# Heads and chunks of a hybrid decoder layer reordered, with one addition chain and one small inverse on GpSimd

## The chip, the cores and the metric

The kernel runs on one core of a Trainium2 chip. The metric is the device time of one launch in microseconds. The kernel before took 1549.87 us, the median of three runs (1549.57 to 1550.96).

## The reference

One decoder layer for a prompt of 16 learned tokens and 512 others, and for eight sampled sequences with a paged cache of 16 pages each. The layer has a gated delta rule branch and a stick-breaking attention branch, then a merge and an FFN. The change touches the two prompt branches alone.

```python
def sb_weights(z, valid):                       # attention, per head
    log_stay = jnp.where(valid, jax.nn.log_sigmoid(-z), 0.0)
    log_after = lax.cumsum(log_stay, axis=z.ndim - 1, reverse=True) - log_stay
    return jnp.where(valid, jnp.exp(jax.nn.log_sigmoid(z) + log_after), 0.0)

def gdn_chunk(S, xs):                           # delta rule, per chunk
    ...
    sol = lax.linalg.triangular_solve(lmat, rhs, left_side=True, lower=True, unit_diagonal=True)
    u, w = sol[..., :DV_A], sol[..., DV_A:]
    v_new = u - jnp.einsum('bhck,bhkv->bhcv', w, S)
    qk = jnp.einsum('bhid,bhjd->bhij', q, k) * decay
    o = jnp.einsum('bhck,bhkv->bhcv', q * jnp.exp(G)[..., None], S) + jnp.einsum('bhij,bhjv->bhiv', qk, v_new)
    S_new = jnp.exp(g_last)[..., None, None] * S + jnp.einsum(
        'bhck,bhcv->bhkv', k * jnp.exp(g_last[..., None] - G)[..., None], v_new)

def gdn_finish(o, z, norm_w):
    o = o * lax.rsqrt(jnp.mean(o * o, axis=-1, keepdims=True) + EPS) * norm_w.astype(F32)
```

## The kernel before

Everything is written by hand: each engine has its own instruction list, and the lists are tied together by waits on semaphores. The order of the work is the order of each list. Most of the span is weights: tiles of 128 output features run on TensorE as three products of split operands (L1044). Between tiles of the input projection stand two stages that are chains.

**Heads** (`attend`, once for each of TensorE, ScalarE, VectorE and GpSimd). Eight heads of the prompt's attention. Keys are cut into five tiles of 128, and each tile's queries are the later ones only, so a head is five pieces (`SB_PIECES`), 1344 columns in three PSUM banks. Per head: TensorE makes the scores (L1126); ScalarE scales them into `zs` (L1668, three buffers) and takes abs, exp and ln of softplus in `es` (one buffer, L1676 to L1680); VectorE finishes softplus into `sps` (L2151, two buffers); GpSimd masks it (`causal`, L2648, five selects); TensorE sums it over later keys (`later_sums`, L1141: a triangular product within a key tile and, for every later key tile, a product with ones); VectorE subtracts the sums from the scores (L2161); GpSimd masks the result (again L2648); ScalarE exponentiates (L1690); TensorE multiplies with the values (`values`, L1152); ScalarE copies out (L1695). TensorE's list is sums(h), scores(h+2), values(h). VectorE's is subtraction(h), some pages, softplus(h+2).

**Pages.** A page is 128 rows of a sampled sequence's key cache, fetched by SyncE. VectorE multiplies it with the query and reduces it in eight instructions, one for each head (`k_page`, L2096). Pages are handed out to fill VectorE's idle time: about 3.75 for each head of the attention, and 16 of the seventh sequence in the chunks, by `CHUNK_PAGES`. In the chunks they use a ring of three buffers, so page p is fetched after page p-3 was used, in SyncE's list, which also holds `get_inverse(c)` (eight loads of 32x32 blocks into the two buffers that GpSimd zeroed for chunk c), `late_page` (a page of the eighth sequence, after a chunk's query products) and `last_inverse`.

**Chunks** (`chunks`, again once per engine). The 528 prompt tokens are four chunks of 128 and one of 16, eight heads each, in groups g of four heads. The 32x32 inverses of the diagonal blocks are made ahead; for each chunk two levels (s = 32, 64) join them into one inverse U (`levels`): product q1 on TensorE (L1315), copy by ScalarE (L1810), product up (L1325, L1329), subtraction on VectorE (L2329, L2330 for 32; L2335 for 64). GpSimd makes the masked inputs (L2768). The 16x16 inverse of the last chunk is made in chunk 1 by VectorE's `invert_last`: 30 dependent instructions on 8 partitions and a copy (L2216, L2219, L2237), and goes through DRAM by `last_inverse`.

For chunk c (d = c + 1) TensorE's list is: state products "ks" with the keys, transposed keys "tk" of d, state products "qs" with the queries, transposed values "tv" of d, new values "vn" (L1359), decay columns "dc" of d, state update "kv", output part "o2", key-query products "kq" of d, the levels of d, transposes of the normalised output "ot" (L1383), read by ScalarE (L1839). "ot" and "qs" use the same PSUM banks. VectorE's list: R (L2358, subtracts "ks"), "kr" and "bv" of d, pages, S, o, the products "qk" of d, then the norm: sum of GpSimd's squares "ss" (L2388), "ms", and, after ScalarE's logarithm and exponential "rl" and "rt" (L1832, L1834), "rq" and "on" (L2395); then the levels of d with their pages. GpSimd's list: level inputs and masks of d, decay rows of c + 2, the squares "sq" of c (L2802), zeroing for c + 2 (L2723, L2724).

## Time and profile before

| | us |
|---|---|
| median of three runs | 1549.87 |
| profiled execution | 1550.86 |
| its span | 1548.9 |
| TensorE busy | 1413.1 (91%) |
| VectorE busy | 787.1 (51%) |
| ScalarE busy | 509.5 (33%) |
| GpSimd busy | 147.0 (9%) |
| heads, first sums to last values | 218.3 to 333.4 |
| chunks, loop | 549.7 to 679.5 |

The profiled execution took 1550.86 us, of which the span from the first to the last instruction is 1548.9. Busy times are of one engine over the whole span and overlap. In the rows PE is TensorE, DVE VectorE, ACT ScalarE, POOL GpSimd, and SPq the queue of SyncE, which issues DMAs. In a timeline a row is a run of like instructions with its start and length; in brackets stands how long the engine was idle before it and who ended that. The granted clock is a share of TensorE's full 2.4 GHz.

### The profile page before, as it was taken

What the parts mean: (1) busy time and instruction counts of PE and PEld (TensorE: products, weight loads), DVE (VectorE), ACT (ScalarE), POOL (GpSimd) and SP (SyncE); (2) the same over time, 40 slices, a digit from 0 to 9 for tenths busy, and PEclk for the clock granted to TensorE, in tenths of its full rate; (3) what the DMA queues carried; (4) which work ended last, traced back from release to release, by engine and by line L of the source; (5) the groups of instructions that cost most, each with busy time, mean ns of one, the idle gap of its engine ahead of it and who ended that gap; (6) DMA issues with size and microseconds to landing.
All of it is one profiled execution on the core that took longest, in us unless ns stands there. A gap on an engine that the chain in (4) does not pass through costs nothing.

```text
span 1548.9 us, 28016 instructions
## 1 busy us (share of the span) xinstructions
PE 1413.1 (91%) x10682; PEld 1290.0 (83%) x10682; DVE 787.1 (51%) x2988; ACT 509.5 (33%) x776; POOL 147.0 (9%) x228
## 2 busy tenths in 40 slices
PE   5979978879999787879997999998989999999998
PEld 3979965568988787769776788898989999999998
DVE  4578747657889878752344421344243333232222
ACT  3323345526844322220223432223232222222212
POOL 1000012122320533100320000000000000000000
PEclk9999999989999878976989999998999999999999
DMA  9359944534532423429989999923223333333222
GB/s 324 97 190 294 296 171 165 163 124 135 172 101 70 123 61 103 122 65 279 313 306 314 362 344 311 308 76 117 82 59 92 96 96 91 88 92 89 76 76 79
DMA packets 254473, 252.56 MB, mean 163 GB/s; under 512 B 22433, under 2 KB 215083, under 8 KB 254309
## 3 DMA queue, kind: packets, MB, share of 16 engines
q1 hardware_dynamic: 254341, 250.79, 50.8%
q8 instruction: 84, 1.38, 0.4%
q14 instruction: 48, 0.39, 0.1%
HBM read 235.66 MB, written 15.29 MB: 162 GB/s over the span
## 4 chain that ended last, share of the span: by engine, by line
PE 76%; DVE 9%; DMA 4%; ACT 4%; POOL 3%; issue 2%; SPq 1%; POOLq 0%; ACTq 0%; DVEq 0%
PE ps L1044 54%; PE ps L1073 3%; PE ps L1141 3%; PE ps L1152 2%; DMA wring<-in_w_ffn_out 2%; PE ps L1425 2%; PE ps L1444 1%; DVE wring L2096 1%; DVE kring L2096 1%; PE ps L1342 1%; PE ps L1085 1%; DVE R L2161 1%; DMA out_rec_sample<-R 1%; POOL R L2802 1%; POOL R L2648 1%
## 5 line engine op out<-in xcount | busy, mean ns | idle before, releaser
L1044 PE MATMUL ps<-obT_split,wring_split 128*128 128x268 f32 (+2 forms) x1296 | 265.2, 286 | 0.0
L1044 PE MATMUL ps<-obT_split,qv_split 128*128 128x260 f32 (+2 forms) x1040 | 219.1, 292 | 12.7 <-DVE wring_split L587 11.2
L587 DVE TENSOR_TENSOR wring_split<-wring,vring_split 128x1024 fp32r<-128x1024 f32 (+1 forms) x92 | 110.5, 1201 | 236.0 <-ACT vring_split L581 236.0
L1044 PEld LDWEIGHTS ps<-obT_split,wring_split 128*128 128x128 f32 (+1 forms) x1296 | 202.0, 189 | 0.7
L1044 PE MATMUL ps<-obT_split,vring_split 128*128 128x260 f32 (+1 forms) x960 | 197.6, 287 | 0.8 <-issue 0.8
L1044 PE MATMUL ps<-xn_split,vring_split 128*128 128x260 f32 (+1 forms) x960 | 194.6, 284 | 4.1 <-DVE obT_split L601 4.1
L1044 PEld LDWEIGHTS ps<-obT_split,qv_split 128*128 128x128 f32 (+1 forms) x1040 | 162.1, 190 | 37.0 <-issue 34.4
L1044 PE MATMUL ps<-xn_split,qv_split 128*128 128x260 f32 (+2 forms) x912 | 187.0, 287 | 0.0
L1614 ACT ACTIVATE R<-ps 128x520 f32<-128x520 f32 (+1 forms) x86 | 52.5, 611 | 372.5 <-PE ps L1044 372.5
L587 DVE TENSOR_TENSOR wring_split<-wring,qv_split 128x1024 fp32r<-128x1024 f32 (+1 forms) x73 | 91.7, 1256 | 146.4 <-ACT qv_split L581 146.3
L1044 PEld LDWEIGHTS ps<-xn_split,vring_split 128*128 128x128 f32 x960 | 149.0, 190 | 4.9 <-issue 4.2
L1044 PEld LDWEIGHTS ps<-obT_split,vring_split 128*128 128x128 f32 x960 | 148.9, 189 | 3.0 <-issue 2.6
L581 ACT ACTIVATE vring_split<-wring 128x1024 fp32r<-128x1024 f32 (+1 forms) x92 | 95.3, 1036 | 150.1 <-DMA wring<-in_w_ffn_out 107.3
L1044 PEld LDWEIGHTS ps<-xn_split,qv_split 128*128 128x128 f32 (+1 forms) x912 | 141.8, 189 | 0.7
L1044 PE MATMUL ps<-xn_split,wring_split 128*128 128x260 f32 x704 | 142.0, 283 | 0.0
L1044 PE MATMUL ps<-R_split,vring_split 128*128 128x260 f32 x592 | 111.9, 286 | 2.4 <-DVE rows_split L601 2.4
L2096 DVE CUSTOM_DVE_ANT_0 kring<-kring,qv 128x128 f32<-128x128 f32 x480 | 110.1, 297 | 5.5 <-DMA kring<-in_cache_k 5.2
L1044 PEld LDWEIGHTS ps<-xn_split,wring_split 128*128 128x128 f32 x704 | 109.6, 190 | 0.0
L581 ACT ACTIVATE qv_split<-wring 128x1024 fp32r<-128x1024 f32 (+1 forms) x73 | 76.1, 1042 | 61.5 <-PE ps L1044 24.9
L1044 PE MATMUL ps<-R_split,wring_split 128*128 128x260 f32 x464 | 93.7, 283 | 0.0
L1044 PEld LDWEIGHTS ps<-R_split,vring_split 128*128 128x128 f32 x592 | 88.9, 192 | 2.6 <-DVE rows_split L601 2.6
L1044 PEld LDWEIGHTS ps<-R_split,wring_split 128*128 128x128 f32 x464 | 72.1, 190 | 0.0
(391 smaller groups left out, 2191.4 us busy)
## 6 DMA issues: line engine op xcount, KB each, us to landing
wring<-in_w_in SPq DMA_DIRECT2D x72, 512.0 KB, 5.7
kring<-in_cache_k SPq DMA_DIRECT2D x64, 512.0 KB, 5.0
vring<-in_cache_v SPq DMA_DIRECT2D x64, 512.0 KB, 6.2
kring<-in_cache_v SPq DMA_DIRECT2D x64, 512.0 KB, 5.6
wring<-in_w_ffn_in SPq DMA_DIRECT2D x44, 512.0 KB, 3.8
vring<-in_cache_k SPq DMA_DIRECT2D x24, 512.0 KB, 4.8
R<-in_cache_k SPq DMA_DIRECT2D x24, 512.0 KB, 7.0
wring<-in_cache_k SPq DMA_DIRECT2D x16, 512.0 KB, 3.7
```

The costliest lines, as they stand in the source:

```text
L581: nc.scalar.activation(fr(w_part(w_high(p), p)), w_part(wring[:, p % RING, :], p), ACT.Copy).then_inc(w_hi, 1)
L587: nc.vector.tensor_tensor(fr(w_part(wlo[:, p % RING, :], p)), w_part(wring[:, p % RING, :], p), w_part(w_high(p), p), ALU.subtract).then_i ...
L1044: last = mm(ps[0:m, 2 * (t % 2) + i, 0:n], fr(w), fr(x[k][:, a + i * n:a + i * n + n]), start=(k == 0 and w is w_h and x is hi), stop=(k = ...
L1073: m = mm(ps[32 * i:32 * i + 32, 6 + half, :], dw[:, b, 32 * g:32 * g + 32], (vring, kring)[r][:, i, 512 * half:512 * half + 512], start=(g ...
L1085: m = mm(ps[:, 5, h:h + 1], vacc[:, 0, h * P:h * P + P], selv[:, h:h + 1], start=True, stop=True)
L1141: m = mm(ps[:, 3 + bank, col + q - a:col + b - a], lhs[:, :], sps[:, h % 2, f:f + b - q], start=(j == 0), stop=(j == len(parts) - 1))
L1152: m = mm(ps[:, 6, q - META:LP - META], vtok[0:n, k, h * P:h * P + P], zs[h % 3][0:n, f:f + LP - q], start=(k == 0), stop=(k == TT - 1))
L1342: m = mm(at_head(bank + g, c, h, P), cT[:, block + h, t0:t0 + n], S[:, h, :], start=True, stop=True)
L1425: m = mm(ps[:, 4, 2 * r:2 * r + 2], st[:, r, :], cT[:, h:h + H + 1:H, LP + b], start=True, stop=True)
L1444: m = mm(ps[:, 4 + i % 2, r4 * P:r4 * P + P], masked_keys(i)[:, r4, :], vrow[:, :], start=True, stop=True)
L1614: go(halves(dst[:, first_token(t):TOKENS]), pair(t, m), func).then_inc(act_read, 1)
L2096: m = v.tensor_tensor_reduce(kh, kh, qh, 1.0, 0.0, ALU.mult, ALU.add, dz[:, b % 4, p * H + h:p * H + h + 1])
```

## The change

In the heads TensorE's list becomes sums(h+1), values(h), scores(h+3), with sums(0) and scores(2) ahead of the loop. VectorE does softplus(h+1) right after subtraction(h). ScalarE does the exponential of h+1 ahead of the copy of h. GpSimd adds up the tails: for each key tile the masked softplus of all later tiles beyond the next (`tail_sums`, five additions of 16, 128, 128, 16 and 144 columns per head), so that TensorE's products with ones are at most two for each piece.

In the chunks the output norm of c is finished behind parts of the levels of d: VectorE's list has the level of 32 ahead of "ss" and "ms", and the level of 64, with one page, between "ms" and "rq"; ScalarE's has the level copies ahead of "rl" and "rt". TensorE's "ot" of c moves behind "ks" and "tk" of the next iteration. The small inverse moves from VectorE in chunk 1 to GpSimd in chunk 2, ahead of the squares. SyncE's `last_inverse` moves behind page 15. Pages are handed out anew. Counts of semaphore values follow.

```diff
--- before.py
+++ after.py
@@ -171,9 +171,10 @@
 
-CHUNK_PAGES = {("levels", 0, 0): [0], ("levels", 0, 1): [1], ("levels", 0, 2): [2, 3], ("kv", 0): [4],
-               ("levels", 1, 1): [5], ("levels", 1, 2): [6, 7], ("levels", 2, 1): [8], ("levels", 2, 2): [9, 10],
-               ("kv", 2): [11], ("levels", 3, 1): [12], ("levels", 3, 2): [13, 14], ("kv", 3): [15]}
+CHUNK_PAGES = {("levels", 0, 0): [0], ("levels", 0, 1): [1], ("levels", 0, 2): [2], ("kv", 0): [3, 4],
+               ("levels", 1, 1): [5], ("levels", 1, 2): [6], ("kv", 1): [7, 8], ("levels", 2, 1): [9],
+               ("levels", 2, 2): [10], ("kv", 2): [11, 12], ("levels", 3, 1): [13], ("levels", 3, 2): [14],
+               ("kv", 3): [15]}
 
...
@@ -664,17 +666,17 @@
             more = d < TT
-            pe_keys += (both(c, "ks") if c else []) + (both(d, "tk") if more else []) + (both(c, "qs") if c else [])
+            pe_keys += (both(c, "ks") if c else []) + (both(d, "tk") if more else [])
+            pe_keys += both(c - 1, "ot") + both(c, "qs") if c else []
             pe_keys += (both(d, "tv") if more else []) + both(c, "vn") + (both(d, "dc") if more else [])
-            pe_keys += both(c, "kv", "o2") + (levels_pe(d) if more else []) + both(c, "ot")
-            act_keys += (both(c, "qs") if c else []) + both(c, "vn") + (both(d, "dc") if more else [])
-            act_keys += [(c, "rl"), (c, "rt")]
+            pe_keys += both(c, "kv", "o2") + (levels_pe(d) if more else both(c, "ot"))
+            act_keys += both(c - 1, "ot") + both(c, "qs") if c else []
+            act_keys += both(c, "vn") + (both(d, "dc") if more else [])
             act_keys += [k for s in LEVELS[d] for k in both(d, ("q1", s))] if more else []
-            act_keys += both(c, "ot")
+            act_keys += [(c, "rl"), (c, "rt")] + (both(c, "ot") if not more else [])
             dve_keys += (both(c, "R") if c else []) + (both(d, "kr", "bv") if more else []) + both(c, "S", "o")
-            dve_keys += both(d, "qk") if more else []
-            dve_keys += [(c, "ss"), (c, "ms"), (c, "rq"), (c, "on")]
-            dve_keys += levels_32(d) + levels_64(d) if more else []
+            dve_keys += both(d, "qk") + levels_32(d) if more else []
+            dve_keys += [(c, "ss"), (c, "ms")] + (levels_64(d) if more else []) + [(c, "rq"), (c, "on")]
             pool_keys += both(d, *[("L", s) for s in LEVELS[d]], "cm") if more else []
@@ -945,11 +947,11 @@
                     chunk_pages(8, 10)
-                    last_inverse()
                     get_inverse(3)
                     chunk_pages(10, 14)
                     late_page(1)
                     chunk_pages(14, PAGES)
+                    last_inverse()
                     late_page(2)
@@ -1128,18 +1130,22 @@
                 def later_sums(h):
-                    pe.wait_ge(s_msp, h + 1)
+                    pe.wait_ge(s_msp, 4 * h + 4)
                     if h == 0:
                         pe.wait_ge(tok_a, 2 * H)
                     else:
                         pe.wait_ge(s_arg, h)
                     for kt, a, b, bank, col in SB_PIECES:
-                        parts = [(tri_ge, kt, a)] + [(ones, k2, max(a, P * k2)) for k2 in range(kt + 1, TT)
-                                                     if P * k2 < b]
-                        for j, (lhs, k2, q) in enumerate(parts):
-                            f = sb_at(k2, q)[2]
-                            m = mm(ps[:, 3 + bank, col + q - a:col + b - a], lhs[:, :],
-                                   sps[:, h % 2, f:f + b - q], start=(j == 0), stop=(j == len(parts) - 1))
+                        f, near, far = sb_at(kt, a)[2], P * (kt + 1), P * (kt + 2)
+                        parts = [(tri_ge, a, b, sps[:, h % 2, f:f + b - a])]
+                        if near < b:
+                            e, f = min(far, b), sb_at(kt + 1, near)[2]
+                            parts.append((ones, near, e, sps[:, h % 2, f:f + e - near]))
+                        if far < b:
+                            parts.append((ones, far, b, tails[kt + 1]))
+                        for j, (lhs, q, e, rhs) in enumerate(parts):
+                            m = mm(ps[:, 3 + bank, col + q - a:col + e - a], lhs[:, :], rhs,
+                                   start=(j == 0), stop=(j == len(parts) - 1))
                     m.then_inc(s_c, 1)
@@ -1157,11 +1163,14 @@
                 head_tokens(vbT, 1, 7)
+                later_sums(0)
+                scores(2)
                 for h in range(H):
-                    later_sums(h)
-                    if h + 2 < H:
-                        scores(h + 2)
+                    if h + 1 < H:
+                        later_sums(h + 1)
                     values(h)
+                    if h + 3 < H:
+                        scores(h + 3)
 
@@ -1399,6 +1408,7 @@
                     if c:
+                        outputs(c - 1)
                         state_products(c, "qs")
@@ -1408,7 +1418,7 @@
                         levels(c + 1)
-                    outputs(c)
+                outputs(TT - 1)
                 pe.wait_ge(g_act, ACT_AT[4, "ot", 1])
@@ -1679,20 +1689,27 @@
 
+                def weights(h):
+                    act.wait_ge(s_marg, h + 1)
+                    go(zs[h % 3], zs[h % 3], ACT.Exp).then_inc(s_w, 1)
+
                 head_tokens(vtok, 1, 5)
                 softplus(0)
                 head_tokens(vtok, 1, 6)
                 scaled(1)
                 head_tokens(vtok, 1, 7)
                 softplus(1)
+                scaled(2)
+                weights(0)
+                softplus(2)
                 for h in range(H):
-                    act.wait_ge(s_marg, h + 1)
-                    go(zs[h % 3], zs[h % 3], ACT.Exp).then_inc(s_w, 1)
-                    if h + 2 < H:
-                        scaled(h + 2)
-                        softplus(h + 2)
+                    if h + 1 < H:
+                        weights(h + 1)
                     act.wait_ge(s_av, h + 1)
                     nc.scalar.copy(qbT[:, h, META:LP], ps[:, 6, :]).then_inc(s_o, 1)
+                    if h + 3 < H:
+                        scaled(h + 3)
+                        softplus(h + 3)
 
...
@@ -1828,17 +1854,13 @@
                         decay_columns(c + 1)
+                    if c + 1 < TT:
+                        levels(c + 1)
                     after("dve", c, "ms")
                     go(onr[0:n, H:2 * H], onr[0:n, 0:H], ACT.Ln, bias=epsc[0:n, :]).then_inc(g_act, 1)
                     after("act", c, "rl")
                     go(onr[0:n, 2 * H:3 * H], onr[0:n, H:2 * H], ACT.Exp, scale=-0.5).then_inc(g_act, 1)
-                    if c + 1 < TT:
-                        levels(c + 1)
-                    for g in G2:
-                        after("pe", c, "ot", g)
-                        go(oaT[:, 4 * g:4 * g + 4, t0:t0 + n],
-                           ps[:, 6 + g, 0:4 * n].rearrange("p (h j) -> p h j", h=4), ACT.Copy,
-                           scale=cols[:, 24:25]).then_inc(g_act, 1)
+                outputs(TT - 1)
 
...
@@ -2161,10 +2182,10 @@
 
+                    if h + 1 < H:
+                        softplus(h + 1)
                     for b, p in K_PAGES["att", 2 * h] + K_PAGES["att", 2 * h + 1]:
                         k_page(b, p)
-                    if h + 2 < H:
-                        softplus(h + 2)
 
...
@@ -2328,11 +2342,19 @@
                         v.tensor_tensor(te, te, product(g, 32, 256), ALU.subtract).then_inc(g_dve, 1)
-                        pages("levels", c, 1 + g)
+                        if g == 0:
+                            pages("levels", c, 1)
+
+                def levels_64(c):
+                    if not LEVELS[c]:
+                        return
+                    pages("levels", c, 2)
+                    n, w, U = chunk(c), chunk(c) // 2, Um[c % 2]
                     for g in G2:
                         after("pe", c, "up", 64, g)
                         ue = odd(U[:, hs(g), :], 64)
-                        v.tensor_tensor(ue, ue, product(g, 64, 0), ALU.subtract).then_inc(g_dve, 1)
+                        v.tensor_tensor(ue, ue, ps[0:n, 2 + g, 0:4 * w].rearrange("p (h b s) -> p h b s", h=4, s=64),
+                                        ALU.subtract).then_inc(g_dve, 1)
 
...
@@ -2361,8 +2384,6 @@
                         value_rows(c + 1)
-                    if c == 1:
-                        invert_last()
                     pages("kv", c)
@@ -2384,18 +2405,19 @@
                         query_products(c + 1)
+                        levels(c + 1)
                     after("pool", c, "sq")
                     v.tensor_reduce(onr[0:n, 0:H], osq[0:n, :, :], AX.X, ALU.add).then_inc(g_dve, 1)
                     after("dve", c, "ss")
                     v.tensor_tensor(onr[0:n, 0:H], onr[0:n, 0:H], rq2[0:n, H * c:H * c + H], ALU.mult).then_inc(g_dve, 1)
+                    if c + 1 < TT:
+                        levels_64(c + 1)
                     after("act", c, "rt")
                     v.tensor_tensor(onr[0:n, 2 * H:3 * H], onr[0:n, 2 * H:3 * H], rq[0:n, H * c:H * c + H], ALU.mult)\
                         .then_inc(g_dve, 1)
                     after("dve", c, "rq")
                     v.tensor_tensor(O[0:n, :, :], O[0:n, :, :], per_head(onr[0:n, 2 * H:3 * H], P), ALU.mult)\
                         .then_inc(g_dve, 1)
-                    if c + 1 < TT:
-                        levels(c + 1)
 
@@ -2684,6 +2706,23 @@
 
+            def tail_sums(h):
+
+                pool.wait_ge(s_msp, 4 * h + 1)
+                if h:
+                    pool.wait_ge(s_c, h)
+
+                def row(k, a, b):
+                    f = sb_at(k, a)[2]
+                    return sps[:, h % 2, f:f + b - a]
+                g_.tensor_tensor(tails[3], row(3, 4 * P, LP), row(4, 4 * P, LP), ALU.add).then_inc(s_msp, 1)
+                g_.tensor_tensor(tails[1][:, 0:P], row(1, 2 * P, 3 * P), row(2, 2 * P, 3 * P), ALU.add)
+                g_.tensor_tensor(tails[2][:, 0:P], row(2, 3 * P, 4 * P), row(3, 3 * P, 4 * P), ALU.add)
+                pool.wait_ge(s_msp, 4 * h + 2)
+                g_.tensor_tensor(tails[2][:, P:P + 16], row(2, 4 * P, LP), tails[3], ALU.add).then_inc(s_msp, 1)
+                pool.wait_ge(s_msp, 4 * h + 3)
+                g_.tensor_tensor(tails[1][:, P:P + 144], row(1, 3 * P, LP), tails[2], ALU.add).then_inc(s_msp, 1)
+
             pool.wait_ge(ab_d, AB_G)
@@ -2693,9 +2732,28 @@
                     causal(zs[h % 3], NEG, s_marg)
+                if 0 <= h + 1 < H:
+                    tail_sums(h + 1)
                 if h + 2 < H:
                     pool.wait_ge(s_sp, h + 3)
                     causal(sps[:, h % 2, :], 0.0, s_msp)
+
+            def invert_last():
+
+                X3, A3, T3 = (b.rearrange("p (i j) -> p i j", j=16)
+                              for b in (X4, PA4, dsuf[0:H, :, :].rearrange("p a n -> p (a n)")))
+                pool.wait_ge(x_ok, 2)
+                for j in range(15):
+                    lo, w = 15 - j, j + 1
+                    pool.wait_ge(x_st, 62 + 2 * j)
+                    g_.tensor_tensor(T3[:, 0:lo, 0:w], A3[:, j + 1:16, j:j + 1].to_broadcast([H, lo, w]),
+                                     X3[:, j:j + 1, 0:w].to_broadcast([H, lo, w]), ALU.mult).then_inc(x_st, 1)
+                    pool.wait_ge(x_st, 62 + 2 * j + 1)
+                    g_.tensor_tensor(X3[:, j + 1:16, 0:w], X3[:, j + 1:16, 0:w], T3[:, 0:lo, 0:w], ALU.subtract)\
+                      .then_inc(x_st, 1)
+                pool.wait_ge(x_st, 62 + 30)
+                g_.tensor_copy(PA4.rearrange("p (j i) -> p j i", i=16), X4.rearrange("p (i j) -> p j i", j=16))\
+                  .then_inc(x_ok, 1)
 
@@ -2793,6 +2851,8 @@
                     decay_rows(c + 2, gm).then_inc(g_pool, 1)
+                if c == 2:
+                    invert_last()
                 after("dve", c, "o", 0)
```

## Rows read from the trace of the kernel before

**Rows 1.** Busy time of two heads: length, engines, clock, DMA share, GB/s

```profile
247.36:260.72 13.36, 11.15 (x52) 7.77 (x51) 10.35 (x71) 7.34 (x9) 2.69 (x10) 1.00 0.48 152
...
274.08:289.00 14.92, 12.71 (x52) 8.41 (x51) 10.35 (x68) 8.83 (x11) 2.69 (x10) 0.89 0.50 158
```

**Rows 2.** TensorE's timeline, heads: start, length, instructions, wait before

```profile
218.28 2.08 PE L1141 MATMUL ps<-R,tri_ge 128*128 128x512 f32 x2 [3.05 <-POOL R L2648]
...
234.92 1.67 PE L1141 MATMUL ps<-R,ones 128*128 128x400 f32 x8
...
239.66 2.70 PE L1126 MATMUL ps<-R 128*128 128x512 f32 x10
...
244.61 2.82 PE L1152 MATMUL ps<-R 128*128 128x512 f32 x10 [2.25 <-ACT R L1690]
...
312.97 5.33 PE L1152 MATMUL ps<-R 128*128 128x512 f32 x10 [4.76 <-ACT R L1690]
```

**Rows 3.** VectorE's timeline, heads

```profile
239.84 1.68 DVE L2161 TENSOR_TENSOR R<-R,ps 128x512 f32<-128x512 f32 x3 [1.45 <-PE ps L1141]
...
241.44 0.28 DVE L2096 CUSTOM_DVE_ANT_0 kring<-kring,qv 128x128 f32<-128x128 f32 x1
...
250.23 1.56 DVE L2151 SCALAR_TENSOR_TENSOR R<-R 128x1344 f32<-128x1344 f32 x1 [1.56 <-ACT R L1680]
```

**Rows 4.** GpSimd's timeline, heads

```profile
238.46 1.20 POOL L2648 TENSOR_SCALAR_AFFINE_SELECT R<-R 128x112 f32<-128x112 f32 x5 [8.66 <-DVE R L2151]
...
241.67 1.53 POOL L2648 TENSOR_SCALAR_AFFINE_SELECT R<-R 128x112 f32<-128x112 f32 x5 [2.02 <-DVE R L2161]
```

**Rows 5.** Busy time between new values of successive chunks

```profile
552.25:582.41 30.16, 28.42 (x217) 28.23 (x217) 24.13 (x93) 7.84 (x19) 11.80 (x10) 0.86 0.17 45
...
582.41:619.73 37.32, 29.53 (x219) 29.34 (x217) 31.86 (x115) 8.46 (x22) 11.86 (x10) 0.82 0.36 106
...
619.73:646.26 26.53, 24.56 (x218) 23.90 (x217) 21.03 (x99) 8.45 (x22) 3.53 (x4) 1.00 0.21 61
...
646.26:665.54 19.28, 13.48 (x122) 11.57 (x120) 11.72 (x43) 4.64 (x14) 2.38 (x3) 0.82 0.69 219
```

**Rows 6.** TensorE's timeline, chunks

```profile
542.52 1.06 PE L1281 MATMUL ps<-ident,R 128*128 128x128 f32 x8 [2.73 <-DVE vring L2335]
...
565.76 1.10 PE L1325 MATMUL ps<-R,vring 128*128 128x64 f32 x8 [1.74 <-ACT R L1810]
...
601.08 1.97 PE L1325 MATMUL ps<-R,vring 128*128 128x64 f32 x8 [7.79 <-ACT R L1810]
...
658.77 1.97 PE L1383 MATMUL ps<-ident,qv 128*128 128x128 f32 x8 [5.80 <-DVE qv L2395]
```

**Rows 7.** VectorE's timeline, chunks

```profile
541.97 0.74 DVE L2335 TENSOR_TENSOR vring<-vring,ps 128x256 f32<-128x256 f32 x2
...
573.20 1.16 DVE L2096 CUSTOM_DVE_ANT_0 wring<-wring 128x128 f32<-128x128 f32 x1 [1.36 <-DMA wring<-in_cache_k]
...
583.68 0.16 DVE L2216 TENSOR_TENSOR dsuf<-lvl 8x15 f32<-8x15 f32 x1
...
592.88 0.36 DVE L2237 COPY lvl<-lvl 8x256 f32<-8x256 f32 x1
```

**Rows 8.** GpSimd's instructions by shape: count, busy us, mean ns

```profile
L2703 POOL TENSOR_TENSOR R<-tri_gt,small 16x128 f32<-16x128 f32 x2 | 0.8, 410 | 0.0
...
L2827 POOL TENSOR_TENSOR R<-R,lvl 128x64 f32<-128x64 f32 x1 | 0.3, 331 | 0.0
```

**Rows 9.** GpSimd's timeline, start of the kernel

```profile
4.18 1.20 POOL L2648 TENSOR_SCALAR_AFFINE_SELECT selv<-selv 128x8 f32<-128x8 f32 x4
```

**Rows 10.** SyncE's timeline, chunks: its DMA issues

```profile
565.01 3.79 SPq L852 DMA_DIRECT2D vring<-xdram  x8
...
569.55 1.50 SPq L729 DMA_DIRECT2D wring<-in_cache_k  x2
...
583.96 1.48 SPq L729 DMA_DIRECT2D wring<-in_cache_k  x2
```

20 lines of the change are left out of this document (12 added, 8 removed).

## The prediction

> **What bounds the kernel now.** I read busy time by stretch first. A head of the attention holds 11.15 us of TensorE work in 13.36 [rows 1]; the four loop intervals of the chunks hold 96.0 in 113.3, at a granted clock of 0.82 to 1.00 [rows 5]. The change touches only these two stages, so I read each as a chain: every step waits for TensorE or is waited for by it, and what counts is which wait ends last.
>
> *Heads.* Where the clock fell to 0.89 a head took 14.92 [rows 1]. The timelines [rows 2 to 4] show a circle: suffix sums on TensorE 5.70 (233.96 to 239.66), the subtraction on VectorE 1.60 (239.84 to its next instruction at 241.44), GpSimd's masks 1.53 (from 241.67), ScalarE's exponential 1.4 (243.2 to 244.61), values 2.82, and the next sums. During the three middle steps TensorE has only the scores, then waits 2.2.
>
> *Chunks.* From one chunk's new values (L1359) to the next it is 30.16, 37.32, 26.53 and 19.28 us [rows 5]. The third ran at full clock with 24.6 us of TensorE work. The waits [rows 6]: 2.73 before the loop, for VectorE's pages; 1.74 in chunk 0 (and again in 2) and 7.79 in chunk 1, for ScalarE's copies of the level products, which stand in its queue behind the root of the output norm, and that behind VectorE; 5.80 in chunk 3 for the output norm itself. The 7.79 is the small inverse: 31 instructions on VectorE from 583.68 to 593.2 [rows 7].
>
> **The change, part 1: heads.** TensorE's order becomes sums(h+1), values(h), scores(h+3). The exponential leaves the circle. But softplus(h+1) on VectorE now follows the subtraction of head h, and GpSimd masks softplus(h+1), then masks the arguments of h, then adds the tails, all before sums(h+1). The circle is now:
> - sums: a piece's ones products fall from 1440 columns to 832 in 7 matmuls for 10. The row of the 832 columns takes 1.67 us, 2.0 ns a column with its last one still draining [rows 2]; at 1.8 to 2.0, 608 columns are 1.1 to 1.2, so 5.70 becomes 4.6.
> - subtraction 1.60; softplus 1.56 and 0.07 to GpSimd [rows 3, 4].
> - two masks of five instructions. Beside VectorE's pages one took 1.53, alone 1.20 [rows 4]. VectorE is always in its pages now: 1.5 each, 3.0 (bounds 2.4 and 3.1).
> - tails: five additions of 16, 128, 128, 16 and 144 columns, none of them in the trace. Nearest are GpSimd's products of 64 columns, 0.33, and of 128, 0.41 us [rows 8]; the line through them puts 16 columns at 0.27 and 144 at 0.43. That makes 0.27+0.41+0.41+0.27+0.43 = 1.8, and 0.3 for a self-wait and for VectorE beside it: 2.1. Bounds 1.5 and 3.0.
> - hand-overs 0.1.
>
> Sum 13.0 (11.8 to 14.0) against 13.36: almost the same circle. VectorE's 1.60+1.56 and 3.75 pages of 1.7 us (8 instructions 0.21 apart) [rows 3] are 9.5 and fit beside it.
>
> TensorE now does 11.15 - 1.1 = 10.05 us a head and waits 3.0 in one piece, right ahead of the sums, which are on the circle. After waits of 3.05 and 4.76 it ran at the low clock of 1.2 GHz each time [rows 2], after the usual 2.2 in one head of six [rows 1]: the values took 5.33 instead of 2.82, that head 1.56 more. So a fall costs 1.6 to 2.5. I take two heads in three at 1.7: circle 14.1.
>
> Ends: sums(0), begun at 218.28 at low clock, now waits 1.8 for its tails and ends near 226.7; sums(1) begins 13.0 - 4.6 = 8.4 later, after a wait of 5.6 since no values exist yet to fill it, at low clock: it ends at 241.8 instead of 239.66 (+2.1). Five circles make 70.5 instead of 4 x 13.36 + 14.92 = 68.4 (+2.1). The last one before holds the wait of 4.76 and the values of 5.33, 15.8 in all; now, without scores to fill it, 13.0 and 1.7 to 2 of low clock (-0.9). Behind it the last values wait 4.5, as before, and are less slow (-1.2). Heads: **+2**, -3 if the clock never falls, +7 if in every head.
>
> **Part 2: chunks.** Times are counted from the chunk's new values, V.
> - Before the loop page 3 moves behind: 1.7 off the 2.73. **-1.7**, on the path.
> - Chunk 0. The wait of 1.74 and its low clock (567.6 to 574) go. Late next is the norm: VectorE now needs page 6 before levels_64 and the norm's end, and page 6 still waits for SyncE's eight block loads, 3.79 us, released by GpSimd's zeroing at 565.0; it landed at 573.20, V+20.95 [rows 7, 10]. Then page 1.7, levels_64 0.74 [rows 7], scaling 1.4: norm at V+24.85. TensorE begins the levels at V+9.8, as before; five groups of 16 products (q, up and its T half, q, up) take 1.8 each, so it is through them at V+19.0 (0.2 for copies), and through state products (1.8) and key transposes (0.9) at V+21.7. It waits 3.1. Then 0.9 output transposes, 0.4 because the query products overwrite the banks that ScalarE must empty (0.69 a copy), products 1.8, transposes 0.87: next V at 28.9, plus 0.8 of low clock, against 30.16: **-0.5**.
> - Chunk 1. The inverse (9.5) is gone from VectorE, but page 8 is now wanted in "kv"; it is issued behind late page 0, 1.5 after V [rows 10], lands near V+6: state update and query products 1 late. Zeroing ends at V+15, block loads 3.8, page 10 issued V+19.7, landed V+23.4; page, levels_64, norm: V+27.3. Next V at 31.3, plus 1.7 low clock after a wait of 5, against 37.32: **-4.3**.
> - Chunk 2. GpSimd runs the inverse from V+5.5, ahead of the square that the norm needs. VectorE's steps took 0.2 to 0.25 from start to start where nothing stalled them. On GpSimd a product of 15 to 64 columns is 0.2 to 0.33 and a self-wait adds 0.1 (four selects of 8 columns, each waiting for the last: 1.20) [rows 9]: 0.4 times 31 is 12.5, bounds 9.5 and 17. The square ends V+19.9, reduce 1.4, page 1.7, levels_64 and norm 2.2: V+25.2 against a slot at V+20.8. Next V 29.2 and 0.9 low clock, against 26.53: **+3.5** (0 to +8). This is the cover that fails: before, nothing stood ahead of this square.
> - Chunk 3. State products go ahead of the wait, but transposes, query products and R follow it. The norm ends at V+12.5 (the wait of 5.80 ended at 658.77, V = 646.26) as before; transposes at low clock and copy 2.0, products 2.5: V+16.9 against 19.28: **-2.4**. SyncE's last_inverse, now behind page 15, waits for GpSimd's result at V+18 of chunk 2, 45 before its use: nothing.
>
> What goes is that ScalarE's copies stand behind the root; what is late next is the norm. Chunks: **-5.4**, between -19.5 (all page waits and the inverse covered: intervals 26.3, 26.1, 26.1, 16.9 and the 1.7) and +1.
>
> The Trainium skill ("GPSIMD Engine Reference", section 4.1, Engine selection) speaks against both moves to GpSimd: it calls that engine about twice as slow as VectorE for elementwise operations with two inputs. By it the inverse, 7.2 us on VectorE without the three instructions that something else held up, would be 14.4 and chunk 2 at +5.4, the sum -1.5. The trace agrees in direction: a GpSimd product of 64 columns takes 0.33 us [rows 8], the first ones of VectorE's inverse 0.16 [rows 7].
>
> **Sum.** +2 - 5.4 = -3.4. The profiled execution took 1550.86 around a span of 1548.9; that is 1.0 above the median of 1549.87. I forecast from the median: 1546.5. Later stages are weights at TensorE's pace and shift whole.
>
> **Rivals.**
> 1. *The chunks' gain comes through whole*: pages landed in time, inverse covered. For: the DMA share is 0.17 to 0.36 in chunks 0 to 2 [rows 5]. Against: page 6 already made VectorE wait 1.36 [rows 7]. 1549.87 + 2 - 19.5 = 1532.
> 2. *The heads gain*: tails 1.5, masks 1.2, waits under 2.2 and thus full clock. Circle 11.8: five are 9.4 shorter, ends 1 us better than before: -10.5, with -5.4: 1534. Against: VectorE's pages run under every mask.
> 3. *Slower*: the wait before the sums drops the clock in each head. Place: L1141; price 1.7 to 2 per head on the circle, so 15; it decides as soon as the wait is 3.05 or more in all heads, as mine is 3.0. Heads +7, chunks -2.5 (each wait there paying too): 1554.4.
> 4. *It moves time only*: the value pages' DMA waits behind 810 us (10 us in all) take back what came early: 1549.
>
> **Chances.** Forecast 0.47 (own range 1541 to 1552), rival 1 0.11, rival 2 0.12, rival 3 0.20, rival 4 0.10. A difference of 0.2% is 3.1 us, about what a measurement can tell here. About half of the forecast's own range lies below it: faster 0.50, same 0.27, slower 0.23. Range 1534 to 1555: it takes in most of rivals 1 and 2 and all of 3.
>
> **What would show it.** Right: L1141 preceded each head by about 3 us released by GpSimd's addition, at low clock in most; L1152 without waits; L1325's waits gone; L1383 waiting on VectorE's scaling in chunks 0 to 3, longest in 1 and 2; VectorE waiting for DMA before page 6 and 10, and for GpSimd in chunk 2. Wrong: a circle under 12.5 or over 14.5, inverse under 9 us, next V of chunks 0 and 1 near 26.

## The result, and the profile after

The changed kernel takes 1556.42 us (median of 5, 1553.55 to 1559.75) against 1549.87 (now five runs, 1549.57 to 1552.21): the ratio is 1.0042, 95% interval 1.0027 to 1.0058. It is slower by 6.5 us, where 3.4 less was forecast. Its profiled execution, 1553.55 us around a span of 1551.8, is the quickest of the five, 2.7 us longer than the one profiled of before; its mean granted clock is 0.938 against 0.943, and the other four had 0.934 to 0.936. So the trace shows the loss at its mildest.

*Heads.* The same view as [rows 2], TensorE's timeline of the changed kernel from the sums of head 1 to those of head 3. Columns: start, busy us, engine, line, operation, operands, count, and in brackets the idle time ahead and who ended it.

```profile
233.76 2.08 PE L1147 MATMUL ps<-R,tri_ge 128*128 128x512 f32 x2 [5.59 <-POOL R L2724]
...
240.98 2.80 PE L1158 MATMUL ps<-R 128*128 128x512 f32 x10
243.71 2.73 PE L1128 MATMUL ps<-R 128*128 128x512 f32 x10
249.28 1.42 PE L1147 MATMUL ps<-R,tri_ge 128*128 128x512 f32 x2 [2.84 <-POOL R L2724]
...
263.56 2.03 PE L1147 MATMUL ps<-R,tri_ge 128*128 128x512 f32 x2 [2.84 <-POOL R L2724]
```

The wait of 2.2 before the values is gone, as said; in its place stands one of 2.84 right before the sums, ended by GpSimd's last addition (L2724). The first products behind it run at the low clock (512 columns twice in 1.4 to 2.1 us, 1.12 at full). The eight sums start at 219.74, 233.76, 249.28, 263.56, 277.83, 291.82, 307.32 and 321.60, a mean circle of 14.55. The windows of two circles answer to [rows 1] (length, then busy us of TensorE, its weight loads, VectorE, ScalarE and GpSimd, granted clock, share and rate of the DMA engines):

```profile
233.76:249.28 15.52, 12.68 (x45) 8.59 (x45) 11.40 (x69) 5.19 (x6) 4.75 (x15) 0.81 0.47 134
249.28:263.56 14.28, 11.44 (x45) 7.66 (x45) 11.40 (x69) 7.35 (x9) 4.75 (x15) 0.88 0.46 142
```

GpSimd's part, its timeline before the sums of head 1: two masks 2.74, then the five additions, 231.59 to 233.70.

```profile
228.88 2.74 POOL L2670 TENSOR_SCALAR_AFFINE_SELECT R<-R 128x112 f32<-128x112 f32 x10 [9.20 <-DVE R L2173]
231.59 0.26 POOL L2718 TENSOR_TENSOR R<-R 128x16 f32<-128x16 f32 x1
...
233.08 0.62 POOL L2724 TENSOR_TENSOR R<-R 128x144 f32<-128x144 f32 x1
```

*Chunks.* The windows from new values to new values, as in [rows 5]:

```profile
553.93:585.57 31.64, 27.89 (x218) 27.49 (x217) 26.98 (x94) 8.04 (x19) 11.90 (x10) 0.89 0.16 43
585.57:620.09 34.52, 29.07 (x219) 28.50 (x217) 24.65 (x99) 8.55 (x22) 11.85 (x10) 0.85 0.36 115
620.09:650.06 29.97, 26.51 (x218) 25.42 (x217) 21.78 (x99) 9.00 (x23) 12.91 (x35) 0.94 0.19 55
650.06:667.06 17.00, 12.96 (x123) 10.97 (x121) 11.55 (x43) 4.66 (x14) 2.38 (x3) 0.90 0.80 249
```

They sum to 113.1, against 113.3 before. Times counted from a chunk's new values are again V+. TensorE's timeline of chunk 0 shows a wait that was not forecast, 3.41 between the two groups of level 64:

```profile
568.24 1.11 PE L1324 MATMUL ps<-vring,kring 128*128 128x128 f32 x8
572.75 1.13 PE L1324 MATMUL ps<-vring,kring 128*128 128x128 f32 x8 [3.41 <-DVE vring L2343]
573.72 3.03 PE L1334 MATMUL ps<-R,vring 128*128 128x64 f32 x16
576.54 3.73 PE L1351 MATMUL ps<-qv,R 128*128 128x128 f32 x16
```

VectorE's timeline and GpSimd's of the same time say why: in the page between the groups of level 32, the three instructions beside GpSimd's level inputs of the next chunk take 1.33 to 1.35 us instead of 0.28.

```profile
567.74 1.35 DVE L2118 CUSTOM_DVE_ANT_0 wring<-wring 128x128 f32<-128x128 f32 x1
569.02 1.34 DVE L2118 CUSTOM_DVE_ANT_0 wring<-wring 128x128 f32<-128x128 f32 x1
570.29 1.33 DVE L2118 CUSTOM_DVE_ANT_0 wring<-wring 128x128 f32<-128x128 f32 x1
571.56 0.28 DVE L2118 CUSTOM_DVE_ANT_0 wring<-wring 128x128 f32<-128x128 f32 x1
...
572.20 0.41 DVE L2343 TENSOR_TENSOR vring<-vring,ps 128x256 f32<-128x256 f32 x1
```

```profile
567.67 3.81 POOL L2826 TENSOR_TENSOR kring<-R,lvl 128x512 f32<-128x512 f32 x3
```

The kernel before had this already: the page instruction of 1.16 at 573.20 in [rows 7] runs beside this product on GpSimd:

```profile
572.95 1.27 POOL L2768 TENSOR_TENSOR kring<-R,lvl 128x512 f32<-128x512 f32 x1 [5.52 <-PE ps L1315]
```

The level inputs of chunk 2 slow the page of chunk 1 in the same way, with the same wait of 3.41. Behind these waits TensorE runs at the low clock, so it is late. VectorE's last step of the norm, and TensorE's output transposes, which need it, in chunks 0 and 1:

```profile
578.54 1.22 DVE L2419 TENSOR_TENSOR qv<-qv,small 128x1024 f32<-128x1024 f32 x1
612.20 1.23 DVE L2419 TENSOR_TENSOR qv<-qv,small 128x1024 f32<-128x1024 f32 x1
```

```profile
581.43 1.04 PE L1392 MATMUL ps<-ident,qv 128*128 128x128 f32 x8
615.95 1.04 PE L1392 MATMUL ps<-ident,qv 128*128 128x128 f32 x8
```

The norm is ready at V+25.8 and V+27.9, and TensorE comes to it only at V+27.5 and V+30.4. It doesn't wait for the norm in these two chunks.

In chunk 2, GpSimd's inverse runs from 625.60 to 637.15 (11.55 us) ahead of the squares. The first and last of its 31 instructions, and TensorE's wait at the output transposes of chunks 2 and 3, answering to the last row of [rows 6]:

```profile
625.60 0.22 POOL L2749 TENSOR_TENSOR dsuf<-lvl 8x15 f32<-8x15 f32 x1
...
636.56 0.60 POOL L2755 COPY lvl<-lvl 8x256 f32<-8x256 f32 x1
637.14 1.88 POOL L2862 TENSOR_TENSOR R<-qv 128x1024 f32<-128x1024 f32 x1
```

```profile
644.23 1.10 PE L1392 MATMUL ps<-ident,qv 128*128 128x128 f32 x8 [2.59 <-DVE qv L2419]
645.66 3.58 PE L1351 MATMUL ps<-qv,R 128*128 128x128 f32 x16 [0.34 <-ACT R L1837]
662.56 1.61 PE L1392 MATMUL ps<-ident,qv 128*128 128x128 f32 x8 [4.04 <-DVE qv L2419]
```

Where the 2.9 us of span sit: the heads end 2.5 later (the tile behind them begins at 336.79, before at 334.24), the stage of the chunks begins 3.2 later (521.86 against 518.64) and ends 3.1 later (689.85 against 686.75). The chunks gained nothing. Behind them nothing changed. By the medians the loss is 6.5; what the slower runs lose on top of this trace, no trace shows.

### The profile page after: what moved, and what is told of

Same layout as the page of the kernel before. It is cut to its first block, busy times and chain, and to the rows that moved or that the text cites. A ratio compares the mean times of both kernels' runs of the same rounds, so it can differ in the third digit from the quotient of the medians.

```text
span 1551.8 us, 27968 instructions
## 1 busy us (share of the span) xinstructions
PE 1412.0 (91%) x10634; PEld 1287.6 (83%) x10634; DVE 788.6 (51%) x2957; ACT 510.0 (33%) x776; POOL 173.0 (11%) x299
## 4 chain that ended last, share of the span: by engine, by line
PE 73%; issue 7%; DVE 6%; POOL 5%; DMA 4%; ACT 4%; SPq 2%; POOLq 0%; ACTq 0%; DVEq 0%
PE ps L1046 55%; PE ps L1075 3%; DMA wring<-in_w_ffn_out 2%; PE ps L1435 1%; PE ps L1351 1%; POOL R L2670 1%; PE ps L1454 1%; PE ps L1334 1%; PE ps L1087 1%; DVE kring L2118 1%; DVE wring L2118 1%; DMA kring<-in_cache_v 1%; SPq L728 1%; PE ps L1324 1%; PE ps L1029 1%
## 5 line engine op out<-in xcount | busy, mean ns | idle before, releaser
L2118 DVE CUSTOM_DVE_ANT_0 kring<-kring,qv 128x128 f32<-128x128 f32 x480 | 114.6, 306 | 5.2 <-DMA kring<-in_cache_k 5.1
```

Of the source, the lines that this page charges most:

```text
L2118: m = v.tensor_tensor_reduce(kh, kh, qh, 1.0, 0.0, ALU.mult, ALU.add, dz[:, b % 4, p * H + h:p * H + h + 1])
```

## The experiments

My theory at this point was that TensorE's clock sets the price of both stages; the rival was the work itself (GpSimd's additions on the circle; in the chunks the slowed page and the inverse). A kernel's time is the median of its runs, a ratio is to the kernel before on the same chip (1550.06 to 1550.72 us on the four chips used), and 0.001 is 1.55 us.

**Each part alone.** The changed heads (the diff in `attend`, in `weights` and `softplus`, and `tail_sums`) with the chunks of before:

> The changed heads with the chunks of before. Theory A (the loss sits in the heads: each head has a wait of 2.8 us ahead of the sums and the clock falls after it): 3 to 6 us over before, 1553 to 1556, first sums to last values 116 us or more against 115.1 before. Rival B (heads even, the loss sits in the chunks, where the level of 64 waits 3.4 us for VectorE in chunks 0 and 1): within 1 us of before.

Measured: 1557.8 us, ratio 1.0053 [1.0040, 1.0067], on the side of theory A and above its range. Its sums too all fall to the low clock at their start, and its mean circle is 14.57. Its profiled execution, again the quickest, ends the heads 4.6 us later than before (338.83 against 334.24).

The changed chunks (all the other pieces of the diff, the pages and the inverse among them) with the heads of before:

> The changed chunks with the heads of before. Theory A: the chunks' gains and losses cancel, 1548 to 1551. Rival B: 3 us or more over before, 1553 to 1556. My forecast had the chunks at -5.4, which would be 1544.5.

Measured: 1549.18 us, ratio 0.9993 [0.9984, 1.0002]; intervals 31.04, 31.86, 29.46 and 17.94. Theory A held. The heads cost +7.4 by the medians, +8 by the ratio, and the chunks bring about -1; together that is the +6.5 of the change. Against the forecast, +2 and -5.4, both parts missed.

**The heads at full clock.** The changed kernel with idle products, whose result nobody reads, in the wait before the sums:

```
+def filler(k):
+    for _ in range(k):
+        mm(ps[:, 7, :], ones[:, :], vtok[:, 0, 0:512], start=True, stop=True)
...
                 later_sums(0)
                 scores(2)
+                filler(6)
                 for h in range(H):
...
                     values(h)
                     if h + 3 < H:
                         scores(h + 3)
+                    if h + 2 < H:
+                        filler(3 if h + 3 < H else 6)
```

> The changed kernel with idle products into an unused PSUM bank behind each head's scores (3 of 512 columns, 2.6 us a head, 6 where the wait is 5.5). They feed nothing. Theory A: the clock no longer falls ahead of the sums, the circle falls from 14.55 to 13.0 to 13.2, heads 9 to 11 us shorter: 1545 to 1548. Rival: the waits do not set the clock, or the circle is longer for another reason: the filler changes nothing, 1556, or costs its own time.

Measured: 1545.48 us, ratio 0.9968 [0.9955, 0.9980], 11 us under the changed kernel and under before as well; theory A held. TensorE's timeline, one circle, then the circle's window:

```profile
246.65 1.13 PE L1147 MATMUL ps<-R,tri_ge 128*128 128x512 f32 x2 [0.27 <-POOL R L2731]
250.95 2.80 PE L1158 MATMUL ps<-R 128*128 128x512 f32 x10
253.68 2.73 PE L1128 MATMUL ps<-R 128*128 128x512 f32 x10
256.24 2.74 PE L1164 MATMUL ps<-R,ones 128*128 128x512 f32 x6
259.25 1.13 PE L1147 MATMUL ps<-R,tri_ge 128*128 128x512 f32 x2 [0.27 <-POOL R L2731]
```

```profile
246.65:259.25 12.60, 12.33 (x51) 7.75 (x51) 11.40 (x69) 7.36 (x9) 4.75 (x15) 1.00 0.49 164
```

GpSimd's and VectorE's work is the same as in the changed kernel, 4.75 and 11.40 us busy, but the circle is 12.60 instead of 14.28, and the granted clock 1.00 instead of 0.88. Additional work on TensorE made the kernel faster. So the additions on GpSimd, which stand in this circle too, aren't what made the heads slower. In this trace the heads end 8.7 us sooner than before (325.55 against 334.24) while the span is only 4.3 shorter (1544.6): 2.5 of the difference is lost behind the chunks, and no experiment looked at why.

**The additions without the new order.** Before, with only the tails on GpSimd and the shorter sums, and TensorE's old order:

```
                 for h in range(H):
                     later_sums(h)          # new: ones products over the tails
                     if h + 2 < H:
                         scores(h + 2)
                     values(h)              # order as before
```

> The kernel before with one part of the change: the tails on GpSimd and fewer columns in the sums, the order of the heads and the chunks as before. Theory A: GpSimd's additions for the next head run while ScalarE exponentiates and TensorE multiplies, so they leave the circle, and the sums are 1.1 shorter: circle 12.2 to 12.3 instead of 13.36, 7 us off, 1542 to 1544. Rival (the additions hold up GpSimd's masks or VectorE): 1548 or more.

Measured: 1549.82 us, ratio 0.9994 [0.9985, 1.0003]. Theory A missed; the rival's time came, but not by its reason, as the next kernel shows. In its timeline the values of head 0 run at full clock behind their wait of 2.21; from head 1 on the same wait is followed by values at the low clock:

```profile
229.76 2.82 PE L1157 MATMUL ps<-R 128*128 128x512 f32 x10 [2.21 <-ACT R L1695]
232.51 1.13 PE L1146 MATMUL ps<-R,tri_ge 128*128 128x512 f32 x2
241.73 4.47 PE L1157 MATMUL ps<-R 128*128 128x512 f32 x10 [2.21 <-ACT R L1695]
246.12 1.13 PE L1146 MATMUL ps<-R,tri_ge 128*128 128x512 f32 x2
```

The circle is 13.6 (232.51 to 246.12). Before had the same wait of 2.2 in a circle of 13.36 and lost the clock in one head of six [rows 1]; with less work around it, it was lost in each but the first. The tails save 1.4 a head (13.36 less the 11.97 of the next kernel) and the clock takes 1.65 (4.47 less 2.82).

**The same with idle products** between scores and values (2 per head, 5 in the last two):

```
                     if h + 2 < H:
                         scores(h + 2)
+                    filler(2 if h + 2 < H else 5)
                     values(h)
```

> The old order of heads with only the tails on GpSimd and fewer columns, plus idle 512-column products into a spare bank of PSUM between the scores and the values of each head (2 per head, 5 in the last two). Theory (the clock, not the work, sets the circle of a head): sums start every 11.9 to 12.0 us at granted clock 1.00 instead of 13.6, the values of a head take 2.8 us instead of 4.5, eight heads end some 12 us earlier, time 1536 to 1540. Rival (the wait before the values is only one of several causes, the clock falls elsewhere too, or the idle products delay the values): circle 13.3 to 13.6, time 1548 to 1552.

Measured: 1537.26 us, ratio 0.9922 [0.9909, 0.9936]. The theory held. From head 1 on every circle is 11.96 or 11.97 at clock 1.00 (the first, with sums that begin at the low clock as in the kernels beside it, takes 14.83):

```profile
234.04:246.01 11.97, 11.47 (x50) 7.38 (x49) 11.17 (x70) 7.34 (x9) 4.70 (x15) 1.00 0.54 181
```

That is 12.6 us under the kernel with the tails alone by the medians and 11 by the ratios, and 7 to 8 under the changed kernel with its idle products. At full clock the old order has the shorter circle (11.97 against 12.60), since there the additions are not on it: for the head from 246.01 they run from 253.79 to 255.91, beside ScalarE's exponential (253.84, 1.32 us) and the first values. Six circles make 3.8 us of this; 3.1 more come at the end, where the changed kernel with idle products still has a wait of 2.68 without them, ahead of values of 5.30 instead of 2.82.

**Idle products alone**, in the kernel before:

> The kernel before with nothing changed but the idle products between scores and values (2 of 512 columns per head, 5 in the last two). Theory (at full clock its circle is sums 5.6 + subtraction 1.6 + softplus 1.6 + mask 1.2 + 3.3 = 13.4 us, and only one circle in the trace fell to the low clock, at +1.6): six circles of 13.36, values of the last two heads at 2.8 instead of 4.4 us, time 1545 to 1548. Rival (idle products alone bring the whole 12 us, the tails nothing): circle 12.0, 1537 to 1539; other rival (nothing): 1550.

Measured: 1549.66 us, 1541.51 to 1554.86 in 12 runs, ratio 0.9994 [0.9979, 1.0008]. The heads did as the theory said, circles of 13.36 to 13.40 at clock 1.00 behind the first, and the stage of the chunks began 6 us sooner (512.49 against 518.64), but the time is not that of the theory: it is that of the second rival, nothing. The profiled execution gave most of it back in chunk 2, where the wait of 1.73, which before had left the clock at 1.00 throughout the interval, was followed by the low clock (groups of 8 products in 1.91 us, not 1.06):

```profile
626.57 1.46 PE L1330 MATMUL ps<-R,vring 128*128 128x64 f32 x8 [1.73 <-ACT R L1815]
627.82 1.91 PE L1334 MATMUL ps<-vring,R 128*128 128x64 f32 x8
```

The interval took 30.9 instead of 26.5. The same wait with the same neighbours cost nothing in one execution and 4.4 us in another; and within the trace of before, 1.74 was followed by the low clock in chunk 0 and not in chunk 2. That the spread of 13 us over the runs comes from such places is likely, but only this one was seen.

**The chunks.** Three edits on top of the changed chunks with old heads. The page behind the second group of level 32:

```
-                        if g == 0:
+                        if g == 1:
                             pages("levels", c, 1)
```

> The changed chunks with the old heads; VectorE's page of the next levels is taken behind the second group of level 32 instead of between the two groups. Theory (the page, slowed by GpSimd's products of the next chunk's level inputs, makes the second group late): the TensorE waits at the first product of the solution in chunks 0 and 1 (up to 2.1 us with these heads) go, intervals of chunks 0 and 1 become about 30 and 30.5 us instead of 31.0 and 31.9; time 1546 to 1548 against 1549.2 of the changed chunks alone. Rival (what the page no longer delays there it delays behind, in the eviction of the solution or the norm): the waits move on, time 1549 to 1551.

Measured: 1551.21 us, ratio 1.0007 [0.9996, 1.0017]; intervals 30.60, 34.72, 30.00, 16.96. The wait between the groups is gone, and the wait at the output transposes is 3.37 and 6.50 in chunks 0 and 1 instead, and 3.60 in chunk 2. The rival held.

The inverse behind the squares:

```
-                if c == 2:
-                    invert_last()
                 g_.tensor_tensor(osq[0:n, :, :], O[0:n, :, :], O[0:n, :, :], ALU.mult).then_inc(g_pool, 1)
+                if c == 2:
+                    invert_last()
```

> The changed chunks with the old heads; in chunk 2 GpSimd's small inverse is issued behind the squares of the output norm instead of ahead of them. Theory (the norm of chunk 2 waits for the inverse, 11.55 us on GpSimd): the wait before the output products of chunk 2 (2.6 us) goes and the interval of chunk 2 is 26.5 to 27.5 us instead of 29.5, while the inverse, some 3 us later, still comes before its first reader; time 1546 to 1547. Rival (the inverse itself is what chunk 3 waits for): chunk 3 takes 20 to 21 us instead of 17.9 and nothing is gained, 1549.

Measured: 1547.82 us, ratio 0.9985 [0.9976, 0.9994]. The wait of 2.6 at the transposes of chunk 2 is gone, and the next new values begin at 640.39, so chunk 2 takes 26.0. Chunk 3 takes 17.2, so the inverse is not late for it: the rival fell. The time is 1.4 under that of the changed chunks alone, above the theory's range, and the two intervals overlap: what is sure is the trace. Chunks 0 and 1 were 31.64 and 34.51 here, with the wait of 3.4 as in the changed kernel.

Then, with that, the level inputs of chunks 2 and 3 held until VectorE is through level 32:

```
             def levels(c):
+                if c in (2, 3):
+                    after("dve", c - 1, "T", 32, 1)
```

> The kernel with the inverse behind the squares, with one wait more: GpSimd starts the level inputs of chunks 2 and 3 only when VectorE has done the second group of level 32 of the chunk before, so that they no longer lie beside VectorE's page between the two groups. Theory (that page, at 1.3 us an instruction instead of 0.28 beside GpSimd's products, makes the second group late): page instructions back at about 0.3 us, the TensorE wait before the first product of the solution (3.4 us in the trace of the kernel without this wait, in chunks 0 and 1) under 0.5 us, intervals of chunks 0 and 1 about 30 and 31.5 us instead of 31.6 and 34.5, time 1544 to 1546 against 1547.8. Rival (the second group is late for another reason, or the norm takes what the levels give): page instructions fast, yet intervals within 1 us of before the edit, 1547 to 1549.

Measured: 1546.55 us, ratio 0.9972 [0.9962, 0.9982]. VectorE's timeline and TensorE's:

```profile
564.78 0.29 DVE L2103 CUSTOM_DVE_ANT_0 wring<-wring 128x128 f32<-128x128 f32 x1
```

```profile
576.55 1.97 PE L1384 MATMUL ps<-ident,qv 128*128 128x128 f32 x8 [4.73 <-DVE qv L2405]
578.44 3.29 PE L1343 MATMUL ps<-qv,R 128*128 128x128 f32 x16
611.60 1.97 PE L1384 MATMUL ps<-ident,qv 128*128 128x128 f32 x8 [6.01 <-DVE qv L2405]
```

The page is fast again and the wait of 3.41 has gone to 0.23, yet chunks 0 and 1 take 31.89 and 34.61: nothing is gained there. TensorE now waits for the norm until V+26.0 and V+29.2, and the transposes and products behind that wait run at the low clock: 5.9 and 5.5 us to the next new values, where the changed kernel, back at full clock by then, takes 4.1. So the collision on VectorE is real, and taking it away only changes which wait the low clock stands behind. These are single traces: the changed chunks with the old heads, with waits of 0.31 and 1.44 in chunk 1 and the products behind the second at full clock, took 31.86 there. What the kernel gains on the one with the inverse moved, 1.3 us by the medians and 2.0 by the ratios, is within what their intervals leave open. The time lies between theory and rival; the intervals are the rival's.

**Together.** Heads as in the kernel of 1537.26, inverse behind the squares, page behind the second group:

> All of it together: old order of heads with tails on GpSimd, fewer columns and idle products between scores and values; the changed chunks with the page behind the second group and the inverse behind the squares. Theory (heads and chunks add): 12 us from the heads, 1 us of the changed chunks alone, 1 to 2 from the page, 2 to 3 from the inverse: 1531 to 1536. Rival (gains of the chunks are lost again because the tail is bound by the clock or by transfers that don't start earlier): 1538 to 1541, as with the heads alone.

Measured: 1534.3 us (4 runs, 1531.21 to 1538.06), ratio 0.9892 [0.9876, 0.9909], as the theory said. And with the page where the change has it and the later inputs:

> Heads of the old order with tails on GpSimd, fewer columns and idle products; the changed chunks with the inverse behind the squares and the later level inputs, the page at its changed place. Theory (heads -12 and chunks -2.5 to -5 add): 1530 to 1534, below the 1534.3 of the combination with the moved page. Rival: the chunks' part is gone again, 1534 to 1537.

Measured: 1533.92 us (4 runs), ratio 0.9896 [0.9879, 0.9912]: the two cannot be told apart, and 1534 is the border of theory and rival. In both TensorE waits for the norm in chunks 0, 1 and 3. The last kernel leaves that wait and fills it, once VectorE has the output (the first new line):

```
                 def outputs(c):
+                    after("dve", c, "o", 1)
+                    for _ in range((4, 5, 0, 4, 0)[c]):
+                        mm(ps[:, 6, :], ones[:, :], S[:, 0:4, :] ..., start=True, stop=True)
                     after("dve", c, "on")
```

> The best combination (heads in the old order with tails on GpSimd and idle products; changed chunks with inverse behind the squares and later level inputs), and idle products of 512 columns also ahead of the output transposes of chunks 0, 1 and 3 (4, 5, 4), where TensorE waits 4.2, 5.6 and 4.0 us for the norm and runs the transposes and state products behind at the low clock (1.97 and 3.76 us instead of 1.04 and 1.95). Theory (clock alone, the wait stays): 2.7 us gained at each of the three places less some 0.5 us where the idle products end behind the norm: 1526 to 1529. Rival (what runs behind at the low clock has slack, because the value side ends later for another reason, or the norm itself ends later): within 1.5 us of the combination's 1533.9.

Measured: 1527.77 us (5 runs, 1524.8 to 1529.88), ratio 0.9854 [0.9836, 0.9872], the best of all and as the theory said. Windows of chunks 0, 1 and 3, first without, then with the idle products:

```profile
534.19:566.15 31.96, 27.56 (x217) 26.83 (x217) 22.63 (x94) 8.30 (x19) 11.81 (x10) 0.89 0.15 42
566.15:600.78 34.63, 27.11 (x219) 26.23 (x217) 21.31 (x99) 8.77 (x21) 11.76 (x10) 0.90 0.36 115
626.76:644.04 17.28, 12.89 (x122) 10.81 (x120) 11.55 (x43) 4.87 (x15) 2.38 (x3) 0.90 0.79 245
```

```profile
534.77:563.82 29.05, 28.48 (x226) 25.96 (x226) 21.96 (x94) 7.95 (x19) 11.92 (x10) 0.99 0.18 47
563.82:596.90 33.08, 29.35 (x228) 26.05 (x227) 21.36 (x99) 8.54 (x22) 11.76 (x10) 1.00 0.38 119
622.96:638.76 15.80, 15.04 (x131) 11.49 (x129) 11.55 (x43) 4.53 (x15) 2.38 (x3) 1.00 0.87 267
```

The three gain 2.9, 1.5 and 1.5 us, 5.9 in all; the medians differ by 6.2. In chunk 0 the norm is also ready earlier, at V+24.8 instead of V+25.5, so of the 2.9 the clock gives back 2.2; in chunk 1 it gives 1.7. The theory had 2.2 at each place, 6.6 in all. So the low clock behind the norm's wait has about that price, and the rival, slack behind that wait, falls. No kernel has these idle products with the collision left in.

## Why the prediction was wrong

The forecast was 1546.5 us. The measured time is nearest to rival 3, which stood at 1554.4 with a chance of 0.20. Two steps of the forecast failed: in how many heads the clock falls, and where TensorE stands in chunks 0 and 1 when the norm is ready. Behind both is the low clock after a wait.

- **The circle of a head.** Summed to 13.0 at full clock; with the clock held it is 12.60. Sums 4.3 (said 4.6), masks 2.74 (3.0), tails 2.1 (2.1), subtraction and softplus as said. "-3 if the clock never falls" is about what the idle products showed: -4.9 for the changed kernel with them, of which the chunks are -1; these products also fill waits at the ends, which the -3 did not count on.
- **"I take two heads in three at 1.7"**: this step failed. The count was wrong: all eight sums ran at the low clock from their first products or from just behind them. The price was right for most (12.60 to 14.28 is 1.7), but two circles took 15.50 and 15.52, 2.9 each. The mean was 14.55 instead of 14.1 in the quickest run, and alone the heads cost +7.4 to +8 instead of +2. The case "+7 if in every head" was the true one, and rival 3 had place (the sums' wait) and price. Its condition was too high: 3.05 was asked for, 2.84 was enough, and in the kernel with tails alone 2.21. Why two circles lost 2.9 is open.
- **Ends of the heads.** Said +2.1 to the end of sums(1), +2.1 for five circles, -2.1 behind; the quickest run had +1.3, +3.9 and -2.7, so its +2.5 in all is near the +2 by luck. With the changed heads alone the trace has +0.7, +3.8 and +0.1: there sums(7) and the last values ran at the low clock. The rest of the medians' loss is in neither trace.
- **Before the chunks' loop**: -1.7 said, -1.5 found.
- **Chunks 0 and 1: TensorE through its work at V+21.7, then waiting 3.1 for the norm (5 in chunk 1)**: this step failed too. The norm was about as late as said (V+25.8 and V+27.9, said V+24.85 and V+27.3), but TensorE came later still, at V+27.5 and V+30.4. The term put at nothing was GpSimd's level inputs beside VectorE's page: a wait of 3.41, and 3.1 and 4.1 us of low clock in the work behind it (8.7 and 9.7 us, at full clock 5.6). [rows 7] had shown one such page instruction, 1.16 at 573.20. The intervals were 31.6 and 34.5 instead of 29.7 and 33.0, together +3.5.
- **Chunks 0 and 1 without the collision.** With the later level inputs TensorE is there at V+21.3 and waits 4.73, as the forecast drew it, and loses the same time again, because "plus 0.8 of low clock" was too low: the transposes and 16 state products behind the wait run at the low clock, and idle products gave back 2.2 us. For chunk 1 "plus 1.7" was right; there the norm was 1.5 later than said, at V+28.8. With the clock held chunk 0 takes 29.05 (said 28.9) and chunk 1 33.1 (31.3).
- **Chunk 2, the inverse**: 12.5 said, 11.55 found; interval 30.1 said, 29.97 found. That the squares lose their cover was right: with the order turned the interval is 26.0.
- **Chunk 3**: 16.9 said, 17.0 found.
- **Behind the loop** nothing was said; the last new values to the next tile take 22.8 instead of 21.2, at a low clock: +1.6.

With these, -5.4 becomes -5.4 + 3.5 + 0.2 + 1.6 = -0.1 (0.2 from before the loop, 1.6 from behind it), near the -1 of the chunks alone. Taking only the collision away would not have saved the forecast of these chunks, as the kernel without it shows; it takes the held clock as well.

Rival 1 needed the pages in time: VectorE waited 3.60 for page 8 and 1.65 for page 10. Rival 2 needed the full clock and a circle of 11.8; with the clock held the changed order has 12.60. Rival 4, gains taken back behind, has nothing for it: 3.1 of delay at the end of the chunks is 2.9 at the end of the span, and in the last kernel 25.0 us of gain there (661.75 against 686.75) are 25.8.

The Trainium skill ("GPSIMD Engine Reference", section 4.1, Engine selection), by which GpSimd takes about twice as long as VectorE for two inputs, would have had the inverse at 14.4, an estimate. The trace has 11.55 where VectorE needed 9.5 with its three held-up instructions and 7.2 without: 1.2 to 1.6 times, less than the page says. Like for like, a product of 8 x 64 takes 0.30 us there and 0.21 on VectorE.

## What to carry to other kernels

When an engine's wait is taken off the path but moved and joined into one, ask what clock the work behind it gets: count its price for every turn of the loop and for all the work up to where the clock is back; waits of 1.7 to 2.8 us were enough here, not every time. If a wait cannot be removed, filling it with products that nobody reads is a cheap trial; here it gave 11 us in the changed kernel, 11 to 12.6 in the old order with shorter sums and 6 in the chunks, though nothing that could be told in the kernel before. And before mending a stall between two engines, look which wait comes next on the same engine: two of three repairs in the chunks only moved it. Where one engine waits for another, read from the rows of the changed kernel which of the two came last, before saying what binds.

## What the hardware showed that was not expected

- Additional TensorE work shortened the time: 27 idle products brought the circles of the changed heads to a granted clock of 1.00 instead of 0.81 to 0.88, and the kernel from 1556.4 to 1545.5 us.
- Shorter work around an unchanged wait lowered the clock: the wait of 2.2 was followed by a fall in one head of six in circles of 13.4 and in all but the first once the sums were 1.4 shorter.
- The same wait of 1.73 to 1.74 was once followed by a fall and once not, for 4.4 us.
- VectorE's page instruction (128 x 128, multiply and accumulate) takes 0.28 us, and 1.33 to 1.35 beside a 128 x 512 product on GpSimd whose length is 1.27. A product of 128 x 8 on VectorE, begun at 574.10 while GpSimd's fourth ran from 573.96 to 575.23, took 1.15 instead of 0.17. The Trainium skill ("GPSIMD Engine Reference", section 1, Specifications) says that GpSimd shares its way into SBUF with VectorE and that instructions of VectorE with two inputs in SBUF contend with it; both of these have two such inputs, and the trace agrees.
